# Two of four head pairs on the opposite partition half, issued in turn with the others; states added by VectorE

## The reference, cut to what matters

```python
def step(s, inp):                      # RWKV-7, one token, state s is [value, key]
    rt, wt, kt, vt, at, bt = inp
    sa = jnp.einsum('bhvk,bhk->bhv', s, at)
    s = s * wt[:, :, None, :] + sa[..., None] * bt[:, :, None, :] + vt[..., None] * kt[:, :, None, :]
    y = jnp.einsum('bhvk,bhk->bhv', s, rt)
    return s, y
```

## Time and profile before

| | |
|---|---|
| time, median of 3 runs | 1719.72 us (1719.68 to 1719.75) |
| the profiled execution: time, span | 1718.78 us, 1716.9 us |
| TensorE busy | 98% of the span |
| VectorE, ScalarE, GpSimd busy | 53%, 39%, 33% |
| TensorE's granted clock | 0.997 of full |
| the recurrence, layer 0 and layer 1 | from 209.7 and from 1049.6 us, some 175 us each |

### The profile page before, as it was taken

How to read it: one execution, slowest core, us unless ns; L and a number is a source line. 1 busy time by engine, 2 the same in 40 slices (tenths; PEclk the granted TensorE clock), 3 DMA queues, 4 the chain that set the end, 5 groups by cost and what they waited for, 6 DMA issues and landing times.

```text
span 1716.9 us, 42320 instructions
## 1 busy us (share of the span) xinstructions
PE 1683.0 (98%) x19077; PEld 1626.7 (95%) x19077; DVE 910.2 (53%) x1382; ACT 665.4 (39%) x1017; POOL 558.5 (33%) x293
## 2 busy tenths in 40 slices
PE   7999999989999999999999999999899999999997
PEld 7999999879999999999999999998799999999997
DVE  4669534345566504666546883344456662166643
ACT  5444344554433212333343533454534331133323
POOL 5443301112343433334333432012134434343431
PEclk9999999999999999999999999999999999999999
DMA  5223200002222322223322222000022232222331
GB/s 147 63 74 84 69 24 4 4 3 68 76 85 86 98 76 75 87 86 96 83 75 74 74 74 58 10 4 3 20 83 79 86 96 85 71 83 87 92 94 56
DMA packets 218869, 115.51 MB, mean 67 GB/s; under 512 B 9332, under 2 KB 216450, under 8 KB 218690
## 3 DMA queue, kind: packets, MB, share of 16 engines
q1 hardware_dynamic: 218610, 112.79, 22.9%
q10 hardware_dynamic: 80, 0.02, 0.0%
HBM read 109.27 MB, written 3.53 MB: 66 GB/s over the span
## 4 chain that ended last, share of the span: by engine, by line
PE 95%; ACT 3%; DVE 1%; issue 0%; POOL 0%; DMA 0%; DVEq 0%; ACTq 0%
PE ps L591 37%; PE ps L592 37%; PE ps L808 2%; PE ps L812 2%; PE ps L770 2%; PE ps L804 1%; PE ps L783 1%; PE ps L596 1%; PE ps L914 1%; PE ps L874 1%; PE ps L977 1%; PE ps L706 1%; PE ps L931 1%; PE ps L863 1%; PE ps L847 0%; PE ps L888 0%
## 5 line engine op out<-in xcount | busy, mean ns | idle before, releaser
L518 POOL TENSOR_TENSOR wlo<-raw,whi 128x1024 fp32r<-128x1024 f32 (+1 forms) x188 | 508.7, 2706 | 865.1 <-ACT whi L1149 865.0
L1149 ACT ACTIVATE whi<-raw 128x1024 fp32r<-128x1024 f32 (+1 forms) x188 | 209.5, 1114 | 650.0 <-PE ps L592 650.0
L591 PE MATMUL ps<-xh,whi 128*128 128x288 f32 x1120 | 332.9, 297 | 4.2 <-DVE xl L1565 4.2
L592 PE MATMUL ps<-xh,whi 128*128 128x288 f32 x1120 | 331.2, 296 | 0.0
L591 PE MATMUL ps<-xl,whi 128*128 128x288 f32 x1120 | 330.3, 295 | 0.0
L592 PE MATMUL ps<-xl,whi 128*128 128x288 f32 x1120 | 329.0, 294 | 0.0
L591 PE MATMUL ps<-xh,wlo 128*128 128x288 f32 x1120 | 328.8, 294 | 0.0
L592 PE MATMUL ps<-xh,wlo 128*128 128x288 f32 x1120 | 328.7, 294 | 0.0
L591 PEld LDWEIGHTS ps<-xh,whi 128*128 128x128 f32 x1120 | 210.5, 188 | 6.3 <-issue 4.7
L592 PEld LDWEIGHTS ps<-xh,whi 128*128 128x128 f32 x1120 | 210.6, 188 | 0.2
L591 PEld LDWEIGHTS ps<-xh,wlo 128*128 128x128 f32 x1120 | 210.7, 188 | 0.0
(11 more groups left out here) (294 smaller groups left out, 3286.7 us busy)
## 6 DMA issues: line engine op xcount, KB each, us to landing
raw<-in_ffn_w_up SPq DMA_DIRECT2D x88, 512.0 KB, 3.8
raw<-in_w_in SPq DMA_DIRECT2D x52, 512.0 KB, 3.7
raw<-in_ffn_w_down SPq DMA_DIRECT2D x32, 704.0 KB, 4.5
raw<-in_w_out SPq DMA_DIRECT2D x16, 512.0 KB, 3.6
xin<-in_x_prompt SPq DMA_DIRECT2D x4, 512.0 KB, 6.3
out<-xin SPq DMA_DIRECT2D x8, 256.0 KB, 2.9
out<-RW SPq DMA_DIRECT2D x16, 64.0 KB, 2.2
g<-in_rwkv_g SPq DMA_DIRECT2D x2, 256.0 KB, 3.0
```

Of the source, the lines that this page charges most:

```text
L518: e.tensor_tensor(wlo[s][:, 0:width], raw[s][:, 0:width], whi[s][:, 0:width].bitcast(F32), ALU.subtract).then_inc(w_lo[s], 1)
L591: e.matmul(acc(out)[:, 0], lhsT, rhs[:, 0:HT], start=start, stop=stop)
L592: return e.matmul(acc(out)[:, 1], lhsT, rhs[:, HT:TOK], start=start, stop=stop)
L1149: e.activation(whi[s][:, 0:width], raw[s][:, 0:width], ACT.Copy).then_inc(w_hi[s], 1)
```

## The change

- Group B's token-major data (tokens on the partitions) lie on the half opposite to their channels. A product that goes from channels to tokens then reads one half and writes the other, and so uses one of the two tiles off the diagonal. `heads(q)` now issues four products in turn, in the order A even, A odd, B even, B odd, each on a tile of its own. In the levels of the inverse group B swaps halves at each level.
- Front steps are no longer split into A and B: one `edges`, one `gram`, one `tokens`, five `level`s for all four pairs. A level now adds the running inverse on TensorE, as a product with the identity; ScalarE copies group B's results and VectorE group A's, one copy of 128x384 each (before: ScalarE copied the powers and VectorE added the inverse, by halves of 128x256 and 128x128).
- The old state of group B can't be added to the same columns of PSUM as the swapped data. Its two terms (into Z and into the output) are computed first, in `solve_z`, to a GLA bank, copied by ScalarE to `carried`, and added by VectorE (`swapped_z`, `swapped_y`). The old states are added by VectorE in `new_state` and `new_gla_state`, each now two instructions for one; L886 and L949 are gone.
- `gla_out` issues 64x64 products in four tiles where it had 64x128 ones. GpSimd's `start_inverse` is gone.

```diff
-PE_F = ["gramA", "gramB", "tokA", "L1A", "tokB", "L1B", "L2A", "L2B", "L3A", "L3B", "L4A", "L4B", "L5A", "L5B"]
+PE_F = ["edges", "gram", "L1", "tok", "L2", "L3", "L4", "L5"]
...
-                def heads(X):
-
-                    for q in range(2):
+                def heads(q, flip=1):
+
+                    for X in range(2):
                         for hp in range(2):
-                            yield 2 * X + q, slice(64 * hp, 64 * hp + 64), q
+                            yield X, 2 * X + q, HALF_ROWS[hp], HALF_ROWS[hp ^ (X & flip)]
...
+                def level(j, k):
+
+                    d = DET[(k + 1) % 2]
...
+                    for q in range(2):
+                        rows = [(X, HALF_ROWS[hp ^ (X & k & 1)], HALF_ROWS[hp ^ (X & (k + 1) & 1)])
+                                for X in range(2) for hp in range(2)]
...
+                            if k < 4:
+                                for X, h, o in rows:
+                                    e.matmul(lv[X][o, q, 0:2], d[h, X, q, 2], d[h, X, q, 0:2], start=True, stop=False)
...
+                            for X, h, o in rows:
+                                mm = e.matmul(lv[X][o, q, 1], ident2[h, :], d[h, X, q, 1], start=False, stop=True)
+                        if k < 5:
+                            for X, h, o in rows:
+                                mm = e.matmul(lv[X][o, q, 2], d[h, X, q, 0], d[h, X, q, 2], start=True, stop=True)
...
                 def solve_z1(i):
 
                     back(ac_b, AC_B, i, "Z")
-                    front(dv_f, DV_F, i, "L5B")
+                    back(dv_b, DV_B, i, "Z")
+                    front(dv_f, DV_F, i, "L5")
+                    front(ac_f, AC_F, i, "L5")
...
-                    gram(j, 0)
+                    edges(j)
                     if i >= 0:
                         solve_z1(i)
-                    gram(j, 1)
+                    gram(j)
                     if i >= 0:
                         solve_z2(i)
                     gla_scores(j)
+                    level(j, 1)
...
-                    tokens(j, 0)
+                    tokens(j)
                     if i >= 0:
                         solve_u(i)
-                    level(j, 0, 1)
-                    tokens(j, 1)
-                    level(j, 1, 1)
+                    level(j, 2)
...
+                def swapped_z(i):
+
+                    step(pe_b, PE_B, i, "Z")
+                    own = pair3(bk[1][:, Z_COL:Z_COL + 2 * C])
+                    if i == 1:
+                        e.tensor_copy(Z[:, 2:4, :], own).then_inc(dv_b, 1)
+                    else:
+                        step(ac_b, AC_B, i, "C")
+                        e.tensor_tensor(Z[:, 2:4, :], carried[:, 0:2, :], own, ALU.add).then_inc(dv_b, 1)
```

More of the change, by code:

```diff
@@ new lines, in gram, with tokens @@
+                    mm.then_inc(pe_f, 1)
+                def tokens(j):
+                    cc = bass.ds(j * C, C)
+                    front(dv_f, DV_F, j, "M")
+                    for a, first in enumerate((RT + NP, 4, 8)):
+                        for q in range(2):
+                            at = (2 * a + q) * C
+                            for X, p, own, tok_half in heads(q):
+                                mm = e.matmul(gr[X][tok_half, at:at + C], RW[own, first + p, cc], ident2[own, :],
+                                              start=True, stop=True)
+                    mm.then_inc(pe_f, 1)
@@ L848, in solve_z1 @@
+                    front(dv_f, DV_F, i, "L5")
+                    front(ac_f, AC_F, i, "L5")
+                    for q in range(2):
+                        for X, p, own, tok_half in heads(q):
+                            mm = e.matmul(column(X, q, U_COL)[tok_half], Tf[i % 2][own, p, :], Z[own, p, :],
+                                          start=True, stop=True)
                     mm.then_inc(pe_b, 1)
@@ L852, in solve_z2 @@
                     back(ac_b, AC_B, i, "Z1")
-                    for p, X, q, o in pairs(zb):
-                        for h in HEADS:
-                            mm = e.matmul(o[h], EK[i % 2][h, p, 0, C:2 * C], Z1[h, p, :], start=True, stop=True)
+                    for q in range(2):
+                        for X, p, own, tok_half in heads(q):
+                            mm = e.matmul(column(X, q, Z_COL)[own], EK[i % 2][tok_half, p, 0, C:2 * C], Z1[tok_half, p, :],
+                                          start=True, stop=True)
                     mm.then_inc(pe_b, 1)
@@ L860, in solve_u @@
                     back(dv_b, DV_B, i, "W")
-                    for p, X, q, o in pairs(zb[:, 256:512]):
-                        for h in HEADS:
-                            mm = e.matmul(o[h], Tf[i % 2][h, p, :], W[h, p, :], start=True, stop=True)
+                    for q in range(2):
+                        for X, p, own, tok_half in heads(q):
+                            mm = e.matmul(column(X, q, U_COL)[tok_half], Tf[i % 2][own, p, :], W[own, p, :],
+                                          start=True, stop=True)
                     mm.then_inc(pe_b, 1)
@@ L869, in outputs @@
                     back(ac_b, AC_B, i, "U")
-                    if i > 0:
-                        back(ac_b, AC_B, i - 1, "Y")
-                    for p, X, q, o in pairs(ys):
-                        for h in HEADS:
-                            e.matmul(o[h], tok[i % 2][h, X, 2, q, :], EK[i % 2][h, p, 1, 0:C], start=True, stop=False)
+                    for q in range(2):
+                        for X, p, own, tok_half in heads(q):
+                            e.matmul(column(X, q, Y_COL)[own], tok[i % 2][tok_half, X, 2, q, :],
+                                     EK[i % 2][tok_half, p, 1, 0:C], start=True, stop=False)
@@ L2007, in _ @@
                 new_state(LAST)
+                swapped_y(LAST)
                 cc = group(N_Y)[1]
```

395 lines of the change are left out of this document (210 added, 185 removed).

## The result

The changed kernel takes 1728.87 us (median of 5 runs, 1727.41 to 1730.77), the kernel before 1719.72 in runs beside it: ratio 1.0053, 95% interval 1.0038 to 1.0068. It is 9 us slower, where 66 us less were forecast.

The account below looks back on a forecast made before the run. TensorE's rate through small products was taken to bound the recurrences. Savings of 29.3, 3.3 and 1.2 us, less 1 given back, make 32.8 a layer, 65.6 in two: 1719.7 - 65.6 = 1654, range 1638 to 1700.

Parts of the forecast that it names:

- I take 0.06 us for four instructions of 64 columns, so 0.12 for a quad: Recurrence products on four tiles: four products (eight instructions) take 0.12 us, between 0.108 and 0.234.
- the 0.88 that was named as a sign: Sign that the forecast is right: gram's 32 instructions take about 0.88 us.
- Streaming sets the pace: TensorE in the recurrences: doubling the columns doubles the time, 0.058 us for two 64-column instructions, 0.11 for two of 128.
- TensorE's work in a plain turn: Turn 3 of the recurrence: products sum to 16.0 us before (17.52 shown) and 11.1 after.
- a floor on starts: Rival for the recurrences: TensorE can't be fed fast enough, four products cost 0.18 us, time 1690; chance 14%.
- The waits for `swapped_z` behind `scale_y`: Starts of turns after group ends: solve_z1 waits 3.45 us in turns 5 and 7, 2.8 in turn 3, 0.5 in turn 1.
- Both ends of a layer: Turn -1 takes 10.5 us for 13.74, 3.3 saved; outputs of the last chunk shrinks from 2.8 to 1.2, 1.2 saved.
- The walk of copies and crossings: A plain turn walked step by step with copies and semaphores: 12.2 us for 17.52, waits costing 1.1.
- The old states added by VectorE: State additions in a turn: VectorE's extra instructions (2 x 0.41 us) cost only the wait before the next solve_z.
- The clock: A clock below 1.00 behind the 3 us waits would cost time; no size was counted.
- The slower rival: Recurrence tiles that share rows take turns, four products cost 0.234 us, and the kernel ends slower at 1740; chance 8%.

Follow-up runs that it names:

- Run 7: The changed kernel with exponentials and scalings moved behind the next turn's copies (1703.63 us), now with group A's inverse added by VectorE: 1682.27 us.
- experiment 2: The kernel before, with the old states added by VectorE alone and their products with the identity gone: 1712.50 us, ratio 0.9952.
- experiment 8: The kernel before with a burst of 256 unused 128-column products ahead of each layer's last solve_z: 13.9 us on four tiles, 27.9 on two.
- experiments 5, 9 and 10: The changed kernel with gram's 128-column products split into 64 columns (1732.29 us), or with 16 (1729.82) or 32 (1724.91) unused products ahead of each layer's recurrence.
- the burst on four tiles: The kernel before with 512 unused 64x64 products ahead of each layer's last solve_z: 27.5 us on four tiles (layer 0), 29.9 on two (layer 1).
- experiment 1: The changed kernel with all products back on the two diagonal tiles, number and order of instructions kept: 1801.09 us, ratio 1.0468.

## Why the prediction was wrong, step by step

- *"I take 0.06 us for four instructions of 64 columns, so 0.12 for a quad"*: right. `tokens` runs at 0.116, the burst of 128 columns at 13.9 / 64 = 0.217 (0.22 taken), and `gram`'s 32 matmuls in turn 3 take the 0.88 that was named as a sign.
- *"Streaming sets the pace", and so "TensorE's work in a plain turn" is 11.1 us*: **this step failed.** It priced each product by its columns and took instructions to be free. Supply gives 256 in about 3.6 us. Turn 1 has 560 matmuls, 1120 instructions with their loads, 15.9 us at 14.2 ns; it takes 16.6, and the 11.8 forecast for it was never to be had. The rival "a floor on starts" was of the right kind, and it had 14%; but its floor was on single starts (0.18 for a quad), while TensorE starts quads at full speed and then stands. In a long run of them a quad costs 16 x 14.2 ns = 0.227 in the mean, next to the 0.234 of before.
- *Missing in the sum*: the instructions that the change adds, net. The new products with the identity in the levels, `edges` apart from `gram`, and `gla_out` in 64x64 make 148 more a turn (1328 matmuls more over 18 turns), 2.1 us at the rate of supply. I had counted the columns of these products and found them cheap on four tiles. Run 7 took 96 instructions a turn away again, for 21 us.
- *The waits for `swapped_z` behind `scale_y`*: right in place and size (2.5, 3.0, 3.6 us) for turns 3, 5 and 7, and forgotten for the last chunk. Worth more than their length: moving the scalings saved 25 us for 18 expected.
- *Both ends of a layer*: wrong. Turn -1 was to fall from 13.74 to 10.5 us and takes 15.1 and 16.3; its 448 matmuls, 896 instructions, need 12.7 us of supply. The last chunk was to be 1.2 us shorter. It takes 12.5 us for 10.2, with the 2.95 us wait for `swapped_z` in it, which the sum put at nothing without a reason.
- *The walk of copies and crossings*: not tested by the time, since supply is slower. The TensorE waits for a copy that the trace shows are small beside the stops. The largest is the one that the walk puts at the end of a turn, `solve_z` for VectorE's sum of the GLA state: 0.6 us each, 7.9 us in 13 times.
- *The old states added by VectorE*: a gain of 8.3 us alone, as experiment 2 has it.
- *The clock*: named and not counted. In the execution whose profile was kept it is at most 15 us of the difference (17.0 - 1.7), from stretches in which TensorE waits; its granted clock was 0.988 over the span, and in the other four executions 0.982 to 0.986. The runs don't separate it from the waits themselves.
- The slower rival was right in sign and wrong in cause: tiles that share rows don't take turns (experiment 8).

In sum: the span was to be 1651 and is 1727, 76 us more. Stops for instructions add up to 64.5 (66.7 - 2.2), but what they cost isn't measured: kernels with 8 to 15 us less of them (experiments 5, 9 and 10) took the same time within 4 us. Six more are the waits in the two last chunks; what is left is the clock and short waits.

What stays open: when exactly a packet is asked for (in the burst on four tiles each was started some 150 to 195 instructions behind the last stop, and the next instruction ran 2.3 to 2.6 us later; on two tiles the packets came every 3.7 us without a stop), and with it how to place a block end on purpose.

## What to carry to other kernels

Count instructions, not only columns: if an edit halves the time that an instruction occupies TensorE, compare the new pace with what the instruction queue delivers (packets of the page's instruction queue against TensorE's instructions, and the closest spacing of those packets). A long stream of small products gains the full factor from more tiles only where each instruction carries enough columns; merge products before spreading them. Part of the gain can be had without that, as experiment 1 shows: with the same instructions four tiles are 72 us faster than two. And look at what stands in the queues of the helping engines when a new dependence on them is made: here the four-tile kernel wins (1682 against 1720) once scalings leave the path and 96 instructions a turn go to VectorE.

## What the runs showed of the hardware

- TensorE got its instructions in packets of 16 KB, 256 at a time, every 3.45 to 3.73 us at the closest in the burst: 14.2 ns an instruction, weight loads counted, in long runs, though 245 matmuls in a row took 3.83 us, 7.8 ns an instruction, where two packets were there.
- Four 64x64 tiles, two of which share rows and two output columns, ran twice as fast as two in a burst that began with packets in hand (13.9 against 27.9 us for 512 matmuls of 128 columns). With 64 columns in a long run it was 27.5 against 29.9 us for 1024.
- A program whose layers have the same instructions need not run alike in them: 178.8 and 184.6 us with 64 stops for instructions, 217.8 and 217.6 with 8.
- Waits were followed by a lower clock: 0.50 to 0.66 granted for 12 us after a stretch of 4.2 us with TensorE busy for 1.4.
